# Key pages asked for between the first weights' chunks, and the first FFN pair's banks taken ahead of the seventh form's preparation

## What is computed

```python
h = rmsnorm(x, p['norm1_w'])
proj = h @ p['w_in']
q, k, v, z, xbc, dt, ga, gb = jnp.split(proj, _split_points(IN_SIZES), axis=-1)
...
attn = stick_breaking_attention(q, k_all, v_all, sb_bias, past).reshape(b, T, ATTN_WIDTH)
...
merged = jax.nn.sigmoid(ga) * (attn @ p['w_pa']) + jax.nn.sigmoid(gb) * (y @ p['w_pb'])
x = x + merged @ p['w_out']
h2 = rmsnorm(x, p['norm2_w'])
x = x + (jax.nn.silu(h2 @ p['w_gate']) * (h2 @ p['w_up'])) @ p['w_down']
```

## Time and profile before

| | |
|---|---|
| median of 3 runs | 1405.22 us (1405.18 to 1407.95) |
| the profiled execution | 1405.4 us, of which the span of its instructions is 1403.9 us |
| busy, share of the span | PE 96%, PEld 90%, DVE 69%, ACT 51%, POOL 19% |
| mean granted clock of TensorE | 0.996 of full speed |

### The profile page before, as it was taken

The page is one execution under the profiler, slowest core; times in us unless marked ns, Lnnn a source line. Parts: engine busy times, 40 slices in busy tenths (PEclk is TensorE's granted clock), DMA queues, the critical chain, the costliest instruction groups (busy, mean ns, idle before and its releaser), DMA issues. The chain is left out here.

```text
span 1403.9 us, 26945 instructions
## 1 busy us (share of the span) xinstructions
PE 1348.2 (96%) x10301; PEld 1256.6 (90%) x10301; DVE 970.3 (69%) x1579; ACT 712.5 (51%) x1282; POOL 264.1 (19%) x467
## 2 busy tenths in 40 slices
PE   5999999999999999999999999999999999999996
PEld 4998777899999997878988887899999999999996
DVE  4664555888853577787687676886899999983221
ACT  4676444777732454665474474535644444452121
POOL 4002233000021523433333324111100000000000
PEclk9999999999999999999999999999999999999998
DMA  4236675122265333334333325362233333323331
GB/s 124 76 84 195 183 215 152 57 71 71 73 160 165 88 98 109 103 89 119 100 111 110 94 79 188 113 192 83 78 101 101 101 91 91 91 72 100 100 96 33
DMA packets 200896, 152.86 MB, mean 109 GB/s; under 512 B 15528, under 2 KB 187584, under 8 KB 200719
## 3 DMA queue, kind: packets, MB, share of 16 engines
q1 hardware_dynamic: 175394, 97.93, 24.7%
q0 software_dynamic: 24992, 52.85, 12.7%
q10 hardware_dynamic: 384, 0.37, 0.1%
HBM read 127.80 MB, written 23.29 MB: 108 GB/s over the span
## 5 line engine op out<-in xcount | busy, mean ns | idle before, releaser
L490 PE MATMUL tile_banks<-x_hi,w_hi 128*128 128x288 f32 (+1 forms) x1232 | 366.6, 312 | 6.3 <-DVE w_lo L464 4.8
L491 PE MATMUL tile_banks<-x_lo,w_hi 128*128 128x288 f32 (+1 forms) x1104 | 309.6, 295 | 0.0
L494 PE MATMUL tile_banks<-x_hi,w_lo 128*128 128x288 f32 (+1 forms) x1232 | 262.2, 294 | 0.0
L490 PEld LDWEIGHTS tile_banks<-x_hi,w_hi 128*128 128x128 f32 (+1 forms) x1232 | 231.4, 188 | 19.6 <-issue 8.5
L464 DVE TENSOR_TENSOR w_lo<-w_raw,w_hi 128x1024 fp32r<-128x1024 f32 (+2 forms) x125 | 150.6, 1204 | 104.4 <-ACT w_hi L458 102.7
L491 PEld LDWEIGHTS tile_banks<-x_lo,w_hi 128*128 128x128 f32 (+1 forms) x1104 | 207.4, 188 | 5.0 <-issue 3.6
L494 PEld LDWEIGHTS tile_banks<-x_hi,w_lo 128*128 128x128 f32 (+1 forms) x1232 | 197.2, 187 | 0.4
L458 ACT ACTIVATE w_hi<-w_raw 128x1024 fp32r<-128x1024 f32 (+2 forms) x125 | 129.5, 1036 | 98.8 <-PE tile_banks L494 94.2
L491 PE MATMUL tile_banks<-f_lo,w_hi 128*128 128x288 f32 x352 | 98.5, 294 | 0.0
L1113 POOL DMA_DIRECT2D out_y_prompt<-y_tok x8 | 6.2, 778 | 385.8 <-ACT y_tok L2329 373.0
L2217 ACT ACTIVATE w_hi<-sum_raw 128x512 fp32r<-128x512 f32 x71 | 44.9, 634 | 59.9 <-PE spare_bank L1686 22.0
(11 more groups left out here) (495 smaller groups left out, 3697.3 us busy)
## 6 DMA issues: line engine op xcount, KB each, us to landing
w_raw<-in_w_in SPq DMA_DIRECT2D x68, 512.0 KB, 3.9
k_page<-in_cache_k SPq DMA_DIRECT2D x64, 128.0 KB, 2.5
v_page<-in_cache_v POOLq DMA_DIRECT2D x64, 128.0 KB, 2.9
old<-in_state_ssm POOLq DMA_DIRECT2D x32, 256.0 KB, 3.5
out_ssm_sample<-old POOLq DMA_DIRECT2D x32, 256.0 KB, 3.0
w_raw<-in_w_pb SPq DMA_DIRECT2D x16, 512.0 KB, 3.6
w_raw<-in_w_down SPq DMA_DIRECT2D x16, 512.0 KB, 3.9
gates_dram<-gate_out POOLq DMA_DIRECT2D x22, 288.0 KB, 2.9
```

The source lines that it names most:

```text
L490: nc.tensor.matmul(out, wh, xh[:, HALVES[h]], start=start and k == 0, stop=False, skip_group_check=onto)
L491: nc.tensor.matmul(out, wh, xl[:, HALVES[h]], start=False, stop=False, skip_group_check=onto)
L494: mm = nc.tensor.matmul(out, wl, xh[:, HALVES[h]], start=False, stop=stop and k == last, skip_group_check=onto)
```

## The change

Two things. **In the first stretch** the request for the page table, and SP's wait for it, move from behind chunk 12 to behind chunk 1, and the eight key pages of units 1 and 2 are asked for one at a time behind chunks 3 to 10. **In the FFN**, for pair 0 alone, VectorE does `take_u2(0)` and `take_u3(0)` in step 2 instead of steps 3 and 4, and `form_add(6)`, the preparation of the seventh form, comes behind them in step 2 instead of standing in step 1.

```diff
+            def load_key(u, k):
+
+                x = units[u]
+                n = page_number(x) + k
+                if n >= K_SLOTS:
+                    eng.wait_ge(sem("k_turned"), 2 * (n // PART - 1))
+                eng.dma_start(k_page[:, n % K_SLOTS, :], cache_k[0, bass.ds(page_of(eng, x, k), 1)].rearrange("o p h d -> p (o h d)")).then_inc(sem(f"k_page_in{n // PART % (K_SLOTS // PART)}"), 16)
+
             for c in range(N_FIRST):
                 load_chunk(eng, first_src(c), c, width=P if c < N_FIRST - 1 else NH)
-            eng.dma_start(pages_sb[:, :], page_table.rearrange("b p -> (b p)").rearrange("(o n) -> o n", o=1)).then_inc(sem("pages_in"), 16)
-            eng.wait_ge(sem("pages_in"), 16)
...
+                if c == 1:
+                    eng.dma_start(pages_sb[:, :], page_table.rearrange("b p -> (b p)").rearrange("(o n) -> o n", o=1)).then_inc(sem("pages_in"), 16)
+                    eng.wait_ge(sem("pages_in"), 16)
+                if 3 <= c < 3 + K_SLOTS:
+                    load_key(1 + (c - 3) // PART, (c - 3) % PART)
...
-            for u in (1, 2):
-                load_keys(u)
...
-                if q == 3:
-                    take_u2(p)
-                if q == 4:
-                    take_u3(p)
+                if q == 3 or step == 2:
+                    if step != 3:
+                        take_u2(p)
+                if q == 4 or step == 2:
+                    if step != 4:
+                        take_u3(p)
                 if q == 5:
                     take_g0(p)
                 if q == 6:
                     take_v1(p)
-                if step + RING < N_FORMS and (step + RING) % 7 in (1, 2, 3, 6):
+                if step == 2:
+                    form_add(step + RING - 1)
+                if step != 1 and step + RING < N_FORMS and (step + RING) % 7 in (1, 2, 3, 6):
                     form_add(step + RING)
                 if step + RING - 1 < N_FORMS:
                     form_lo(step + RING - 1)
```

More of the change, by code:

```diff
@@ L750, in first_src, with load_keys @@
                 return w_in[0, :, COL_DT:COL_DT + NH].rearrange("(t p) n -> p t n", p=P)
+            def load_keys(u):
+                for k in range(PART):
+                    load_key(u, k)
+            def load_key(u, k):
[4 more added lines that the diff above has]
+                eng.dma_start(k_page[:, n % K_SLOTS, :], cache_k[0, bass.ds(page_of(eng, x, k), 1)].rearrange("o p h d -> p (o h d)")).then_inc(sem(f"k_page_in{n // PART % (K_SLOTS // PART)}"), 16)
             for c in range(N_FIRST):
                 load_chunk(eng, first_src(c), c, width=P if c < N_FIRST - 1 else NH)
-            eng.dma_start(pages_sb[:, :], page_table.rearrange("b p -> (b p)").rearrange("(o n) -> o n", o=1)).then_inc(sem("pages_in"), 16)
-            eng.wait_ge(sem("pages_in"), 16)
[L757 to L764, removed]
+                if c == 1:
[3 more added lines that the diff above has]
+                    load_key(1 + (c - 3) // PART, (c - 3) % PART)
             def fill_src(n):
```

## The result

| | before | after |
|---|---|---|
| median of 12 runs each | 1405.83 us | 1409.22 us |
| ratio, 95% interval | | 1.0025 (1.0015 to 1.0036), that is +3.5 us (+2.1 to +5.1) |
| repeated later (32 and 12 runs) | 1406.63 us | 1408.87 us, 1.0013 (1.0003 to 1.0023), +1.8 us (+0.4 to +3.2) |
| the profiled execution | 1405.4 us, clock 0.996 | 1404.49 us, clock 0.998 |

The change makes the kernel slower, by 2 to 3 us over both comparisons. The profiled execution of after happens to be the fastest of its twelve, so nothing can be read from its total; single stretches have to be compared.

The account below looks back on a forecast made before the run. It held TensorE, 96% busy, to be the bound, with VectorE's stream as late. First stretch 0 plus FFN +1.1 us took the 1405.22 us median to 1406.3 us; own range 1405.8 to 1406.9, widened by rivals to 1404.6 to 1408.1.

Parts of the forecast that it names:

- The first stretch, 0: Page table and key page requests moved early: removed waits and added delays were both expected to be worth 0.
- Chunk 3's slack: Weight chunk 3, asked for 9.8 us before use, lands in 3.9 us; 5.9 us of slack hides the early pages.
- Rival 4: First stretch: early pages delay a weight chunk, up to +5.8 us, 1411.0 us; chance 0.03.
- The wait before form 5: FFN: TensorE's 2.19 us wait goes, because u3 of pair 0 ends before form 4 does.
- The new waits: FFN, TensorE: about 0.8 us before form 6 for its low part, 1.9 us before form 7 for ScalarE's Ln.
- Rival 2: FFN: new waits do not come, the chain through form 8 being shorter; form 12 gains 0.44 us, 1404.8 us; chance 0.09.
- Rival 5: ScalarE's table load in the FFN costs some 1.3 us more on the path, 1407.6 us; chance 0.03.
- The drain: ScalarE's table switch: a skill page's drain of about 1.38 us besides the load would make the sum +2.5 us.
- the sum: First stretch 0 plus FFN: form 12 starts at 1021.2 instead of 1020.10, so +1.1 us.
- The fall of the clock: TensorE's clock at forms 7 or 12: harmless at 7, 1.4 to 1.5 us at 12; taken as 0.
- rival 1: Clock falls at form 12, adding 1.5 us: +2.6 us in all, 1407.9 us; chance 0.20.
- Rival 3: All four of TensorE's key page waits go, 3.1 us, giving 1402.1 us; chance 0.05.

Follow-up runs that it names:

- e2: Kernel before with only the first-stretch half of the change (page table and key pages moved); measured 0.9999, -0.1 us.
- r4: Second of four further profiled executions of the unaltered changed kernel; the four took 1406.34 to 1411.53 us.
- r6: Fourth of four further profiled executions of the unaltered changed kernel; the four took 1406.34 to 1411.53 us.
- e1: Kernel before with only the FFN half of the change; measured 1.0017, +2.4 us.
- r5: Third of four further profiled executions of the unaltered changed kernel; the four took 1406.34 to 1411.53 us.
- e9: e5, with SP also reading each unit's four page numbers one unit ahead; against the kernel before, 0.9967, -4.6 us.
- e5: Kernel before with pair 0's two takes and ScalarE's root block in step 2, form_add(6) left in step 1; measured 0.9989, -1.5 us.
- e4: Kernel before with ScalarE's root block in step 2 and nothing moved on VectorE; measured 1.0004, +0.6 us.
- e6: Kernel before with pair 0's u2 and u3 takes in step 2, form_add(6) in step 1, root block in step 4; measured 1.0011, +1.5 us.
- r1: Apparently (label inferred from order) the changed kernel timed again against the kernel before; measured 1.0013, +1.8 us.
- r3: First of four further profiled executions of the unaltered changed kernel; the four took 1406.34 to 1411.53 us.
- e7: e1 with useless matmuls filling the waits, nine before form 7 and ten before form 12; against the kernel before, 1.0010, +1.4 us.
- e8: Kernel before with nine useless matmuls ahead of form 5; measured 0.9997, -0.4 us.

## Why the prediction was right and where it was wrong

**The first stretch, 0: right** within what can be told: e2 shows -0.1 us (-1.5 to +1.1). Chunk 3's slack held, no wait for weights appeared, the waits predicted at 112.10 and 138.95 are at 111.57 and 138.30. Rival 4 didn't come.

**The wait before form 5 is gone: right.** In the changed kernel u3 of pair 0 starts at 1002.19, and form 5 follows form 4 at 1003.71 with no idle time.

**The new waits: right in place and cause.** Predicted 0.8 us before form 6 and 1.9 before form 7; r4 and r6, where TensorE doesn't wait at form 3, show 0.63 and 1.76. Forms 6 and 7 in r4:

```profile
1005.95 0.40 PE L1689 MATMUL tile_banks<-x_hi,w_hi 128*128 128x288 f32 x1 [0.63 <-DVE w_lo L2858]
...
1009.57 0.37 PE L1689 MATMUL spare_bank<-x_hi,w_hi 128*128 128x288 f32 x1 [1.76 <-ACT root L2310]
```

In the other profiles form 3's wait, which I did not foresee, takes form 6's place. The wait before form 12, predicted as 2.2 to 2.4 us, is 1.95, since forms 7 to 11 take 1019.16 - 1.95 - 1008.87 = 8.34 us and not 5 x 1.58 = 7.9. Rival 2 falls with them. Rival 5 falls too: the `Ln` begins 0.02 us behind the table load's end (1006.53 + 1.28 = 1007.81, then 1007.83), with form 7 now waiting for it. The drain of which the Trainium skill speaks (ScalarE: Activation LUTs, section "What ACT_TABLE_LOAD costs") does not show here either.

**The step that failed is the sum, "1021.2 - 1020.1 = +1.1 us"**: the mechanism holds, the term is too small. Form 12 came 1.30 us later than in the profile of before, since `form_add(8)` was 1.69 us late and not 1.55 (behind form 0: 1005.65 - 995.79 = 9.86 and 1005.10 - 993.55 = 11.55). And the profile of before was the slower of its two courses: against the other the same step is 1.64 us. The fall of the clock, taken as 0, is 0 in five of six executions and 1.5 us in one. Together that makes +1.6 to +1.9 us. On the 1405.22 us from which the sum started, a median of three runs, that is 1406.8 to 1407.1 us; on the 1405.83 us of the twelve, 1407.4 to 1407.7. The measured 1409.22 lies beyond either.

**The range was too narrow for what is measured.** It took in rival 1, but not the scatter: single runs of the kernel before lie between 1402.5 and 1410.3 us, and its comparison with itself came out at -0.7 +/- 1.4 us. The repeat's interval (+0.4 to +3.2) and e1's (+1.0 to +3.8) hold 1.6 to 1.9, the first one's (+2.1 to +5.1) doesn't. What the rest of that first comparison was, at least 0.2 us and by its ratio 1.6 to 1.9, stays open; no run shows it to belong to the change. Two things speak for scatter. The kernel before had a median of 1405.83 us there, and 1406.61 to 1406.72 in the three later groups of runs. And the executions of the changed kernel differ ahead of the FFN: r5 has a span of 1410.1 us and the first profile one of 1403.0, and 7.06 of these 7.1 us are there before form 0 starts (at 1000.61 and 993.55).

**Rival 3, the key pages, had its price right and its cause wrong.** The waits are worth some 3 us: -4.6 in e9 against -1.5 in e5, each to within 1.6 us. But neither the first eight requests nor the filler chunks ahead were the reason: it was the reading of page numbers between SP's requests, behind the wait for a free slot.

## What to carry to other kernels

An instruction moved ahead on one engine pays only if nothing queued behind it feeds another engine's queue that the bound waits for; follow the delayed instruction across the engines (here VectorE, ScalarE, VectorE, TensorE) before counting the wait that goes. Two moves can each gain nothing alone and gain together, so a block that sits in the chain (the root) is to be moved with the takes, not after them. And a stretch should be compared from a fixed point in the program, over several profiles: one profile of a kernel may show only one of its courses.

## What the runs showed of the hardware

- **A wait's length alone does not tell whether the clock falls.** It stayed at 1.00 after the 3.35 us in e4, fell to 0.50 after 1.96 us in e6 and r4, and did not after 1.96 us in r5. Stretches of e4, the wait and what followed:

```profile
1007.15:1010.50 3.35, 0.00 (x1) 0.03 (x1) 2.70 (x6) 1.74 (x4) 0.00 (x0) 1.00 0.16 43
1010.50:1013.50 3.00, 3.00 (x23) 3.00 (x24) 3.00 (x6) 1.90 (x2) 0.00 (x0) 1.00 1.09 299
```

- **A fall that no change here touches**, in front of the FFN, where TensorE waits for the merged operand of the product with `w_out` (it lies in the buffer of `conv_acc`). In r5 TensorE waits there and the clock falls:

```profile
942.40 0.37 PE L490 MATMUL tile_banks<-m_hi,w_hi 128*128 128x288 f32 x1 [2.06 <-DVE conv_acc L2826]
```

```profile
943.51:946.92 3.41, 3.41 (x17) 3.41 (x16) 3.26 (x6) 1.73 (x3) 0.00 (x0) 0.50 0.39 117
```

  It came in six of the eight profiles taken on one chip (r1, r3, r5, e7, e8, e9; not r4, r6), after waits of 1.65 to 2.32 us, and in none of the ten others, where two waits (e1, e5) were as long, 1.72 and 1.70 us.
- **One VectorE instruction near the start of the FFN takes over 1.9 us instead of 0.7 to 0.8**, and which one it is decides a wait. In the changed kernel's first profile it is form 3's low part, for which form 3 then waits 0.88 us:

```profile
997.49 1.92 DVE L2858 TENSOR_TENSOR w_lo<-sum_raw,w_hi 128x512 fp32r<-128x512 f32 x1
```

  In that of the kernel before it is the next instruction, and form 3 does not wait:

```profile
1000.35 1.99 DVE L2862 SCALAR_TENSOR_TENSOR x_lo<-x_res,par,x_hi 128x576 fp32r<-128x576 f32 x1
```

  Both courses occur with either FFN (of the changed kernel r4 and r6 go like the second one; e2, whose FFN is that of the kernel before, goes like the first); why it is slow isn't settled.
- **The pace of matmuls differs between executions at full granted clock.** In the same 10 us TensorE does 80 matmuls in the changed kernel's first profile, and 76 in r5:

```profile
430.00:440.00 10.00, 10.00 (x80) 10.00 (x79) 2.74 (x3) 1.85 (x2) 1.07 (x2) 1.00 0.68 192
```

```profile
430.00:440.00 10.00, 10.00 (x76) 10.00 (x75) 3.00 (x3) 1.06 (x1) 1.84 (x4) 1.00 0.60 184
```

  From 417 to 485 us the same 500 matmuls take 67.8 us in both profiles of the kernel before and in r5, and 66.1 to 66.7 us in the other five of the changed kernel. No row here shows why.
